# Other SBUF regions for the second pass's operand slots, the gates' first weights split about 25 steps sooner, and a fourth token sum that is not copied through PSUM

## What is computed

```python
h = rmsnorm(x, g_ffn[i])
x = x + jnp.square(jax.nn.relu(h @ w_ff1[i])) @ w_ff2[i]
gate = jax.nn.sigmoid(rmsnorm(x, g_ple[i]) @ w_ple_gate[i])
x = x + gate * (p[i] @ w_ple_proj[i])
return rmsnorm(x, g_final)
```

## Time and profile before

| | |
|---|---|
| median of 3 runs | 1038.37 us (1037.59 to 1038.87) |
| the profiled execution | 1039.33 us |
| its span, first to last instruction | 1037.5 us |
| mean granted TensorE clock | 0.996 |
| busy: PE / DVE / ACT / POOL | 1024.2 / 764.5 / 529.6 / 499.5 us |
| chain that ended last: PE / DVE / POOL / DMA / ACT | 91 / 3 / 2 / 2 / 1 % |
| DMA | 166.15 MB, mean 160 GB/s |

### The profile page before, as it was taken

One profiled execution on the slowest core, in us unless ns is written; L12 is line 12 of the kernel. 1 busy time (PEld: TensorE's weight loads), 2 busy tenths in 40 slices (PEclk: granted clock), 3 DMA queues, 4 the chain that ended last, 5 costly groups with the idle time before them and its releaser, 6 DMA issues.

```text
span 1037.5 us, 13996 instructions
## 1 busy us (share of the span) xinstructions
PE 1024.2 (99%) x4780; PEld 836.7 (81%) x4780; DVE 764.5 (74%) x906; ACT 529.6 (51%) x944; POOL 499.5 (48%) x350
## 2 busy tenths in 40 slices
PE   9999999999999999999999999999999999999997
PEld 7877788777887888888888878888888888788897
DVE  7988787879797677787787767865776554964658
ACT  7467845554768534334434355443544445553334
POOL 1000061433304887887888547544655456952221
PEclk9999999999999999999999999999999999999999
DMA  9111102101002766767767689577867545500004
GB/s 345 42 38 44 41 2 90 41 28 55 1 11 103 272 236 251 275 242 258 285 243 248 249 311 339 196 230 249 301 225 243 196 144 203 203 1 1 1 1 163
DMA packets 63972, 166.15 MB, mean 160 GB/s; under 512 B 6960, under 2 KB 9008, under 8 KB 61872
## 3 DMA queue, kind: packets, MB, share of 16 engines
q1 hardware_dynamic: 63088, 164.43, 45.2%
q10 hardware_dynamic: 832, 1.05, 0.3%
HBM read 115.12 MB, written 50.33 MB: 159 GB/s over the span
## 4 chain that ended last, share of the span: by engine, by line
PE 91%; DVE 3%; POOL 2%; DMA 2%; ACT 1%; issue 1%; SPq 0%; DVEq 0%; POOLq 0%
PE bank L811 29%; PE bank L813 29%; PE bank L812 29%; DMA right_raw<-u_b 1%; PE bank L926 1%; POOL left_lo L769 1%; PE bank L897 1%; POOL h_lo L769 1%; DVE right_lo L2146 1%; POOL w_lo L698 1%; PE bank L941 1%; PE bank L956 0%; PE bank L881 0%; DMA vec<-in_vectors 0%; DVE h_lo L1675 0%
## 5 line engine op out<-in xcount | busy, mean ns | idle before, releaser
L769 POOL TENSOR_TENSOR left_lo<-left_raw,left_hi 128x512 fp32r<-128x512 f32 x108 | 153.2, 1425 | 141.3 <-ACT left_hi L1525 140.9
L811 PE MATMUL bank<-h_hi,w_hi 128*128 128x512 f32 (+1 forms) x574 | 220.7, 385 | 0.2 <-DVE h_lo L1673 0.2
L812 PE MATMUL bank<-h_lo,w_hi 128*128 128x512 f32 (+1 forms) x574 | 216.9, 378 | 0.0
L813 PE MATMUL bank<-h_hi,w_lo 128*128 128x512 f32 (+1 forms) x574 | 216.9, 378 | 0.0
L2146 DVE TENSOR_TENSOR right_lo<-right_raw,right_hi 128x512 fp32r<-128x512 f32 x108 | 146.7, 1369 | 87.7 <-ACT right_hi L1526 87.4
L811 PE MATMUL bank<-right_hi,left_hi 128*128 128x512 f32 x432 | 168.5, 390 | 3.2 <-DVE right_lo L2146 2.6
L813 PE MATMUL bank<-right_hi,left_lo 128*128 128x512 f32 x432 | 168.1, 389 | 0.0
L812 PE MATMUL bank<-right_lo,left_hi 128*128 128x512 f32 x432 | 168.1, 389 | 0.0
L1525 ACT ACTIVATE left_hi<-left_raw 128x512 fp32r<-128x512 f32 x108 | 68.3, 633 | 149.3 <-DMA right_raw<-u_b 101.8
L811 PEld LDWEIGHTS bank<-h_hi,w_hi 128*128 128x128 f32 x574 | 108.0, 188 | 28.1 <-issue 6.2
L813 PEld LDWEIGHTS bank<-h_hi,w_lo 128*128 128x128 f32 x574 | 108.0, 188 | 20.4
(11 more groups left out here) (249 smaller groups left out, 1828.1 us busy)
## 6 DMA issues: line engine op xcount, KB each, us to landing
right_raw<-u_b SPq DMA_DIRECT2D x76, 256.0 KB, 4.4
left_raw<-w_sums SPq DMA_DIRECT2D x64, 256.0 KB, 3.4
w_raw<-in_w_ff SPq DMA_DIRECT2D x28, 512.0 KB, 5.4
w_set<-in_w_ff SPq DMA_DIRECT2D x26, 512.0 KB, 6.0
w_sums<-w_set SPq DMA_DIRECT2D x13, 1024.0 KB, 3.9
left_raw<-in_w_ff SPq DMA_DIRECT2D x44, 256.0 KB, 3.2
u_b<-u SPq DMA_DIRECT2D x16, 512.0 KB, 3.0
u_t<-usq SPq DMA_DIRECT2D x16, 512.0 KB, 6.4
```

The costliest lines, as they stand in the source:

```text
L769: pool.tensor_tensor(left_lo[o][:, :], left_raw[o][:, :], left_hi[o][:, :], ALU.subtract).then_inc(left_ready, 1)
L811: pe.matmul(o, whi, hh, start=first, stop=False, skip_group_check=onto)
L812: pe.matmul(o, whi, hl, start=False, stop=False, skip_group_check=onto)
L813: return pe.matmul(o, wlo, hh, start=False, stop=last, skip_group_check=onto)
```

## The change

Five things, in the order of the program.

1. The fourth token sum's low part is made from `t_hi` in SBUF, like the third's, without ACT's copy into a bank; ACT and DVE take up sum 3 before sum 4, and DVE puts two tiles of sum 3 ahead of the last block's third and fourth relu. PE's product 0 of block 2 waits for `t_ready[2]` (the last user of the banks), product 6 for `t_ready[4]`.
2. The ring has 16 slots: 0 to 3 in WL and WH, 4 to 7 in T and G, 8 to 11 in Y and Q, 12 to 15 in the token buffers h_hi and h_lo. Steps 0 to 39 use 0 to 7, steps 40 to 63 use 0 to 3 and 8 to 11, steps 64 to 99 use 8 to 15, steps 100 to 111 use 8 to 11, 14 and 15. A table written out at build time gives each step its slot, the step that had it before, and how many loads its semaphore has seen; slots 8 to 15 share the semaphores of 0 to 7, and so SP waits at steps 40 and 64 until ACT has converted all earlier steps.
3. In the last block of the first pass SP issues the loads of steps 3 to 6 behind that of step 2, ahead of the spill of w2's sums, and the spill of `u_b21` before step 8.
4. The late w_ff2 blocks lie in h_lo; p waits for step 39 in place of the spills.
5. The gates' first four halves are loaded at steps 56 to 62, converted at steps 70 to 76, and subtracted at 72 and 76 (POOL) and 80 and 82 (DVE). ACT waits for step 63 before the first of them.

```diff
-NARROW = STEPS - FF_BLOCKS
+EARLY = (0, 1, 2, 4, 5, 6, 7, 3)
+RING_SETS = ((0, EARLY), (40, (0, 1, 2, 3, 8, 9, 10, 11)), (64, (8, 9, 10, 11, 12, 13, 14, 15)),
+             (100, (8, 9, 10, 11, 14, 15)))
+RING_SEM = (0, 1, 2, 3, 4, 5, 6, 7, 4, 5, 6, 7, 0, 1, 2, 3)
+RING_SLOT, RING_BEFORE, RING_COUNT = [], [], []
+for _s in range(STEPS):
+    _slots = [slots for first, slots in RING_SETS if first <= _s][-1]
+    _used = {o: max([t for t, r in enumerate(RING_SLOT) if r == o], default=-1) for o in _slots}
+    _slot = min(_slots, key=lambda o: (_used[o], _slots.index(o)))
+    RING_SLOT.append(_slot)
+    RING_BEFORE.append(_used[_slot])
+    RING_COUNT.append([RING_SEM[o] for o in RING_SLOT].count(RING_SEM[_slot]))
...
-        late_set = (at("late_set0", T, [P, 2, D]), at("late_set1", T + 8 * KB, [P, 2, D]), at("late_set2", G, [P, 2, D]))
-        ring_at = (WL + 8 * KB, WL, WH + 8 * KB, WH, Y, Y + 8 * KB, Q, Q + 8 * KB)
+        late_set = [at(f"late_set{i}", HL + 8 * KB * i, [P, 2, D]) for i in range(len(LATE_SETS))]
+        ring_at = (WL + 8 * KB, WL, WH + 8 * KB, WH, T, T + 8 * KB, G, G + 8 * KB, Y, Y + 8 * KB, Q, Q + 8 * KB)
...
-        for k in (LT, LT + 2):
+        for k in range(0, KD, 2):
...
-                if s >= 8 and ring_before(s) is not None:
-                    step_over(sp, ring_before(s))
+                if RING_BEFORE[s] >= 0:
+                    step_over(sp, RING_BEFORE[s])
...
-            load_step(2)
+            for s in range(2, 5):
+                load_step(s)
+            sp.wait_ge(prod_done, PRODUCTS * 13 + 3)
+            for s in range(5, 7):
+                load_step(s)
             spill_w2((15, 0, 1), w2_sums[6, 1])
             spill_b22((15, 0, 1), u_b22[7, 1])
             sp.wait_ge(w2_spilled, 16 * 13)
-            load_step(3)
+            load_step(7)
             spill_b11((15, 0, 1), u_b11[7, 1])
             spill_t12((15, 0, 1), u_t12[7, 1])
+            spill_b21((15, 0, 1), u_b21[7, 1])
             sp.wait_ge(prod_done, PRODUCTS * 14)
-            load_step(4)
-            sp.wait_ge(spilled_b22, 16 * 16)
-            load_step(5)
-            spill_b21((15, 0, 1), u_b21[7, 1])
-            load_step(6)
-            load_step(7)
             for s in range(8, STEPS):
+                if s == 40:
+                    sp.wait_ge(spilled_b22, 16 * FF_BLOCKS)
+                if s in (40, 64):
+                    sp.wait_ge(right_high, s)
...
-                    sp.wait_ge(w2_spilled, 16 * FF_BLOCKS)
+                    step_over(sp, 39)
...
-                if 64 <= s < 80 and s % 4 == 0:
-                    i = (s - 64) // 4
+                if 56 <= s < 64 and s % 2 == 0:
+                    i = (s - 56) // 2
                     load_half(2 * GATE_FIRST + i, w_ple_gate[i // 2, i % 2])
...
-                if s in (99, 101):
-                    low(2 * GATE_FIRST + (s == 101))
+                if s in (72, 76):
+                    low(2 * GATE_FIRST + (s == 76))
...
-                    pe.wait_ge(t_ready[(4, 2, 1, 3)[i]], LT)
+                    pe.wait_ge(t_ready[(2, 2, 1, 3)[i]], LT)
+                if i == 6:
+                    pe.wait_ge(t_ready[4], LT)
...
-                    if i == 3:
+                    if i > 2:
                         continue
-                    n = LT * (1, 2, 4).index(i) + k
+                    n = LT * (i - 1) + k
...
-            t_high_part(4)
             first_part(1)
+            t_high_part(3)
             for hf in range(2):
                 act.activation(bank[4 + hf][:, :], r_ffn[:, half(hf)], ACT.Copy).then_inc(r_banked, 1)
-            t_high_part(3)
+            t_high_part(4)
...
-                if 98 <= s < 102:
-                    if s == 98:
-                        step_over(act, NARROW - 5)
-                    high(2 * GATE_FIRST + s - 98)
+                if 70 <= s < 78 and s % 2 == 0:
+                    if s == 70:
+                        step_over(act, 63)
+                    high(2 * GATE_FIRST + (s - 70) // 2)
...
             total_head(SS_PLE)
+            step_over(act, 99)
...
-                if i == 3:
+                if i > 2:
                     dve.wait_ge(t_high[i], k + 1)
                 else:
-                    dve.wait_ge(t_banked, LT * (1, 2, 4).index(i) + k + 1)
-                hi = t_hi[i][:, k, :] if i == 3 else bank[T_BANKS[k % 2]][:, :]
+                    dve.wait_ge(t_banked, LT * (i - 1) + k + 1)
+                hi = t_hi[i][:, k, :] if i > 2 else bank[T_BANKS[k % 2]][:, :]
...
+            sum_t3((1, 0, 1))
+            for k in range(2):
+                t_low(3, k)
+            first_relu(1, 2)
+            first_relu(1, 3)
+            for k in range(2, LT):
+                t_low(3, k)
             for k in range(LT):
                 t_low(4, k)
-            sum_t3((1, 0, 1))
-            first_relu(1, 2)
-            first_relu(1, 3)
-            for k in range(LT):
-                t_low(3, k)
...
-                if s in (103, 105):
-                    w_low(2 * GATE_FIRST + 2 + (s == 105))
+                if s in (80, 82):
+                    w_low(2 * GATE_FIRST + 2 + (s == 82))
```

More of the change, by code:

```diff
@@ L270, in build @@
         r_banked, t_banked, step_done = sem("r_banked"), sem("t_banked"), sem("step_done")
-        ring_in = [sem(f"ring_in{i}") for i in range(10)]
+        ring_in = [sem(f"ring_in{i}") for i in range(8)]
         left_high, left_ready, right_high, right_ready = (
@@ L296, in ring_slot @@
         def ring_slot(s):
-            return s % 8 if s < NARROW else 4 + (s - NARROW) % 6
-        def ring_before(s):
-            return s - 8 if s < NARROW else s - 4 if s < NARROW + 4 else s - 6 if s >= NARROW + 6 else None
-        def ring_count(s):
-            if s < NARROW:
-                return 32 * (s // 8 + 1)
-            return 32 * ((NARROW // 8 if ring_slot(s) < 8 else 0) + (s - NARROW) // 6 + 1)
+            return RING_SLOT[s]
         def step_over(eng, s):
@@ L561, in load_step @@
                     src = w2_sums[(n + 1) // 2, (n + 1) % 2, :, k, m * HALF:(m + 1) * HALF]
-                sp.dma_start(left_raw[o][:, :], src).then_inc(ring_in[o], 16)
+                sp.dma_start(left_raw[o][:, :], src).then_inc(ring_in[RING_SEM[o]], 16)
                 if i == 0:
@@ L574, in load_step @@
                     src = u_b21[g, e, :, i // 6, :]
-                sp.dma_start(right_raw[o][:, :], src).then_inc(ring_in[o], 16)
+                sp.dma_start(right_raw[o][:, :], src).then_inc(ring_in[RING_SEM[o]], 16)
             spill_b22((0, 0, 1), u_b22[0, 0])
@@ L1475, in t_high_part @@
                     else:
-                        act.wait_ge(t_ready[(1, 2, 4)[(n - 2) // LT]], (n - 2) % LT + 1)
+                        act.wait_ge(t_ready[1 + (n - 2) // LT], (n - 2) % LT + 1)
                     act.wait_ge(t_high[i], k + 1)
@@ L1523, in step_high @@
                 o = ring_slot(s)
-                act.wait_ge(ring_in[o], ring_count(s))
+                act.wait_ge(ring_in[RING_SEM[o]], 32 * RING_COUNT[s])
                 act.activation(left_hi[o][:, :], left_raw[o][:, :], ACT.Copy).then_inc(left_high, 1)
```

## The result

| | before | with the change |
|---|---|---|
| median of 5 runs | 1038.25 us (1037.59 to 1038.87) | 1032.53 us (1032.36 to 1032.83) |
| the profiled execution | 1039.33 us | 1032.53 us |
| its span | 1037.5 us | 1030.7 us |
| mean granted clock | 0.996 | 0.998 |

The ratio is 0.9946 [0.9932, 0.9961]: 5.7 us less in the medians, 6.8 between the two profiled executions. The forecast was 1030.9 in a range from 1029.6 to 1034.4.

What follows compares the result with a forecast made beforehand. PE was taken as the bound, busy 1024.2 of 1037.5 us. Gains of 3.5 + 1.5 + 2.5 = 7.5 us took the profiled 1039.33 to 1031.8, and 0.96 less for the median gave 1030.9; range 1029.6 to 1034.4.

Steps and rivals of the forecast that it cites:

- signs of being wrong: New wait at product 1 or 4, gap at step 40 or 64, or waits in the last four steps as before.
- (a): Second block's product 0: its late start and the low clock behind it lose 3.79 us; 3.5 won, bounds 2.5 and 3.8.
- product 4's wait: First pass, block 2: PE waits for DVE's add that frees bank 3; 0.3 us taken, between none and 1.3.
- the bound: Product 4's add if POOL delays DVE by 2.55 us and relus are 1.1 late: ends about 345.5, PE waits 1.3.
- The rule of the Trainium skill: VectorE with two SBUF inputs and GpSimd reading SBUF take turns on shared ports; by it alone (a) brings 2.5 us.
- (b): Second pass, step 4: its load, issued late, makes PE lose 1.53 us; earlier issue in new slots wins 1.5.
- (c): Near 884 to 908: PE's waits for POOL and DVE, 2.46 us, go: 2.5 won, bounds 1.0 and 2.5.
- The step from 1031.8 to 1030.9: Whole program: the profiled execution stood 0.96 us above the runs' median, 1038.37, so 0.96 was taken off the forecast.
- The end's waits stay: In the last steps PE's waits remain, so (c) is not won: 1033.4 us; chance 0.10.
- The first pass gains nothing: Product 1 or product 4 of block 2 waits, the clock falls all the same, (a) gone: 1034.4; chance 0.08.
- The fences starve PE: At steps 40 and 64 PE waits for loads; each fence costs 7.6 us, both 15.2: 1046; chance 0.04.
- The change does not do what it says: Product 0 and step 4 start as late as before; under 2 us won, 1036.5 to 1038.4; chance 0.05.

Runs made afterwards that it cites:

- the sum alone: The kernel before with only the fourth sum's new path and order (part 1 of the change); 1036.47 us, ratio 0.9985.
- earlier gates with the short stretch: The change, with steps 96 to 99 in the slots of steps 92 to 95 (four steps of lead, not eight), gates still early; 1033.09 us.
- the late fence: The change, with SP also waiting until PE has ended step 62 before issuing step 64's load; 1039.34 us, ratio 1.0006.
- the square of four kernels: The change with eight steps of lead, gates early 1032.53 us or late 1032.86; with four at steps 96 to 99, early 1033.09 or late 1035.14.
- the run with late gates: The change with the gates' first weights loaded, converted and split at the old steps (64 to 105), in the new ring; 1032.86 us.

## Why the prediction was right, and what was off

**Right in range and sign.** 1032.53 lies 1.6 over the forecast. The terms added up to 7.5, and the stretches that the change touches gained 7.47 against the profile that the terms were read from. But the sum came out by two errors that cancel, which is luck, and the last step was wrong. One of the prediction's own signs of being wrong came, too: a new wait at product 4.

**(a) 3.5 forecast, 2.76 measured.** Product 0 went as said, and the clock stayed up. The term that was mis-sized is product 4's wait: "I take 0.3, nearer the free end, since no more than two POOL instructions are in the way". It measured 1.05, near the other bound of 1.3. Two instructions of POOL were in the way of sum 4, as counted, and cost its four subtractions 2.20 us (4.69 in place of 2.49). Two more had held up sum 3 by 1.71 before, where the bound had 1.1. Each of the two losses is more than the 0.99 us by which the add was late, so undoing either should, as an estimate, end PE's wait; undoing the 2.20 did, and the other was not tried. (The bound's own sum does not close: 342.3 + 2.55 + 1.1 is 345.95 and not "about 345.5", and the prediction does not say what takes up the 0.45.) The rule of the Trainium skill that stood beside the sum, in the page SBUF — State Buffer, section "SBUF: two separate sides", was the better guide; it gave 2.5 for this term. This case's trace agrees in that sum 4 lost 2.20 us over four subtractions beside POOL, and none when POOL waits.

**(b) and (c), 4.0 forecast, 4.71 measured.** Each wait costs more than "about 0.15 more than its idle shows": the matmul behind it is late as well. In the profile before, step 4's second matmul starts 0.31 us after its first and not 0.2266:

```profile
616.89 0.47 PE L811 MATMUL bank<-right_hi,left_hi 128*128 128x512 f32 x1 [1.38 <-DVE right_lo L2146]
617.20 0.39 PE L812 MATMUL bank<-right_lo,left_hi 128*128 128x512 f32 x1
```

That is 0.08 more for each of the five waits, 0.4 together; the other 0.3 stays open, but for one more start, at 878.43, that comes 0.08 late. How much (b) is worth depends on the execution: step 4 lost 1.53 us in the profile of before, 0.66 and 0.77 in the two further ones, and 0.87 with the sum alone.

**(b)'s cause is shown**: with the old issue order in the new slots the wait came back. **(c)'s cause was wrong by half.** "POOL had two gate splits ... in its queue just before" is true, but with eight steps of lead these splits cost nothing. Moving the gates was enough to remove the waits, but it was not needed: the longer ring does it alone, and so do earlier gates with the short stretch (1032.86 and 1033.09 against 1035.14). The prediction saw the crowded queue and not the short stretch at steps 96 to 99, without which it costs nothing.

**The step from 1031.8 to 1030.9** failed. It took off the 0.96 by which the profiled execution stood above the median, as if that excess were spread over the program and would stay. It lay in what the change removes: the lower clock, which some executions of before don't meet, and step 4's wait, 1.53 in that execution and 0.66 and 0.77 in two others. The terms had been measured in that execution, so its excess was in the sum already, and was taken off twice. In 31 runs of before in the first two batches, the eight with a mean clock of 0.996 took 1038.48 us or more, the thirteen with 0.998 took 1038.23 or less; in the nine of the third batch one with 0.996 took 1038.16, and the two with 0.998 took 1037.06 and 1038.09, so the line between them is not sharp. Without this step the forecast is 1031.8; the rest, 0.7, is the wait at 9 us, which happened to be nil in the profile of before.

**The rivals.** "The end's waits stay" fell. "The first pass gains nothing" named the right place, product 4, but the wait was 1.05 and the clock stayed up. "The fences starve PE" fell; its chain was priced within 0.3 us by the late fence. "The change does not do what it says" fell.

## What to carry to other kernels

A profiled execution that is above the median may be so because of the very stall that is costed; subtract either the stall or the excess, not both. When a subtraction on DVE reads two SBUF operands, look for what POOL does in the same microseconds, and if POOL has time to spare, let it wait: here one wait on POOL was worth 1.3 to 1.8 us. A wait with two causes, a short ring and a crowded queue, is not understood from either alone; it took the square of four kernels to see that removing one of them is enough. Where executions of one kernel differ, read the price of a term from more than one of them: step 4's wait was 1.53 us in one profile and half of that in two others.

## What the runs showed of the hardware

The lower clock behind an idle time of PE is not a fixed price. After 1.89 us idle ahead of product 0 the granted clock was 0.57 in one execution and 1.00 in another of the same kernel (336.6 to 339.8 us); after 1.38 us ahead of step 4 it stayed at 1.00 (616.8 to 620 us), and after 1.59 us at 10.45 us, in the run with late gates, too (10.4 to 14 us); after 4.05 at the late fence it was 0.50 for 5.3 us. Where it fell it cost between 1.6 us (271.14 - 269.53, the two further profiles of the kernel before) and 2.5 (the fence).

DVE and POOL side by side both lose: four DVE subtractions with two SBUF operands went from 2.49 to 4.69 us, and two of POOL's from 2.55 to 3.32.
